# Decoder step on one core: one tick later for the samples' first probability transposes and first value product

## The reference, cut to what matters

```python
def forget_attn_prompt(q, k, v, c):          # 16 heads, 528 rows
    ...
        s = jnp.einsum('nqhd,nkhd->nhqk', qb, kp).astype(jnp.float32) * ATTN_SCALE
        s = s + cb[..., None] - ct[:, :, None, :]
        s = jnp.where(kpos[None, :] <= qpos[:, None], s, NEG_INF)
        p = jax.nn.softmax(s, axis=-1)
        return jnp.einsum('nhqk,nkhd->nqhd', p.astype(vp.dtype), vp)

def forget_attn_sample(q, k_new, v_new, c_new, k_past, v_past, c_past):   # 8 samples
    ...
    p = jax.nn.softmax(jnp.concatenate([s_past, s_new], axis=-1), axis=-1)
    out = jnp.einsum('nhqk,nkhd->nqhd', p[..., :past].astype(v_past.dtype), v_past)
    return out + jnp.einsum('nhqk,nkhd->nqhd', p[..., past:].astype(v_new.dtype), v_new)
```

## Time and profile before

| | |
|---|---|
| time, median of 3 runs | 1491.27 us (1487.19 to 1493.64) |
| the profiled execution's own time | 1491.63 us |
| its span in the trace | 1489.8 us |
| PE busy | 1319.4 us, 89% |
| weight loads busy, beside PE | 1025.3 us, 69% |
| DVE, ACT, POOL busy | 34%, 21%, 12% |
| rounds 4 to 7 in the trace | about 780 to 1036 us |
| mean granted PE clock | 0.931 of full |

### The profile page before, as it was taken

The page is one execution under the profiler, slowest core; times in us unless marked ns, Lnnn a source line. Parts: engine busy times, 40 slices in busy tenths (PEclk is TensorE's granted clock), DMA queues, the critical chain, the costliest instruction groups (busy, mean ns, idle before and its releaser), DMA issues.

```text
span 1489.8 us, 37491 instructions
## 1 busy us (share of the span) xinstructions
PE 1319.4 (89%) x16016; PEld 1025.3 (69%) x16016; DVE 499.4 (34%) x1121; ACT 308.5 (21%) x726; POOL 172.5 (12%) x206
## 2 busy tenths in 40 slices
PE   5989999999667889998989999998995899999990
PEld 5888888888534766766665656555454898888870
DVE  4340000000056445464646766664124100000003
ACT  3121000000133221313133543434110001000010
POOL 1012000000031011101021211210000300000002
PEclk9889999999978999999999988999995899999995
DMA  9259999999988759797978996984363599999965
GB/s 304 100 217 319 384 382 383 384 384 392 358 300 294 244 193 364 263 372 252 376 239 268 308 315 229 334 294 153 118 242 118 149 362 387 388 386 384 385 240 197
DMA packets 148138, 437.93 MB, mean 294 GB/s; under 512 B 21383, under 2 KB 52168, under 8 KB 139055
## 3 DMA queue, kind: packets, MB, share of 16 engines
q1 hardware_dynamic: 99319, 367.64, 67.3%
q10 hardware_dynamic: 37744, 38.88, 7.8%
q0 software_dynamic: 10960, 29.80, 6.7%
HBM read 406.38 MB, written 30.24 MB: 293 GB/s over the span
## 4 chain that ended last, share of the span: by engine, by line
PE 48%; DMA 24%; issue 12%; DVE 6%; ACT 3%; SPq 3%; POOL 2%; ACTq 1%; POOLq 0%; DVEq 0%
DMA W<-in_w_up 17%; PE PS L1217 8%; PE PS L1027 5%; PE PS L1352 5%; PE PS L1023 4%; PE PS L1058 4%; PE PS L1053 4%; DMA out_k_prompt<-W 2%; PE PS L964 2%; PE PS L1296 2%; PE PS L1258 2%; PE PS L1304 2%; PE PS L1316 2%; PE PS L956 1%; DMA W<-in_cache_v 1%
## 5 line engine op out<-in xcount | busy, mean ns | idle before, releaser
L1023 PE MATMUL PS<-W,KV 128*32 128x384 f32 x3072 | 344.2, 489 | 16.4 <-DMA W<-in_w_up 12.0
L1027 PE MATMUL PS<-W,KV 128*32 128x128 f32 x3072 | 347.3, 274 | 0.0
L1027 PEld LDWEIGHTS PS<-W,KV 128*32 128x32 f32 x3072 | 334.9, 110 | 1.6
L1217 PE MATMUL PS<-W 128*128 128x256 f32 x768 | 185.4, 397 | 0.7 <-ACT KV L1611 0.7
L2034 DVE TENSOR_TENSOR KV<-KV,PS 128x384 f32<-128x384 f32 x32 | 17.7, 554 | 495.3 <-PE PS L1039 477.2
L1053 PE MATMUL PS<-W,KV 128*32 128x384 f32 x1536 | 176.0, 495 | 5.9 <-ACT KV L1523 5.9
L1058 PE MATMUL PS<-W,KV 128*32 128x128 f32 (+1 forms) x1024 | 176.0, 331 | 0.0
L1217 PEld LDWEIGHTS PS<-W 128*128 128x128 f32 x768 | 149.4, 200 | 32.2 <-issue 10.1
L1023 PEld LDWEIGHTS PS<-W,KV 128*32 128x32 f32 x3072 | 141.8, 110 | 23.4 <-DMA W<-in_w_up 17.9
L2158 DVE STREAM_TRANSPOSE KV<-KV 128x1024 f32<-128x1024 f32 x128 | 154.8, 1225 | 4.5 <-DMA KV<-in_cache_k 4.5
L1058 PEld LDWEIGHTS PS<-W,KV 128*32 128x32 f32 x1024 | 102.7, 110 | 16.5 <-issue 0.7
(11 more groups left out here) (278 smaller groups left out, 1507.5 us busy)
## 6 DMA issues: line engine op xcount, KB each, us to landing
W<-in_w_gate SPq DMA_DIRECT2D x32, 2048.0 KB, 15.7
W<-in_w_up SPq DMA_DIRECT2D x32, 2048.0 KB, 22.2
W<-in_w_down SPq DMA_DIRECT2D x32, 2048.0 KB, 11.7
KV<-in_cache_k SPq DMA_DIRECT2D x256, 256.0 KB, 5.5
W<-in_cache_v SPq DMA_DIRECT2D x128, 512.0 KB, 7.6
yd<-KV ACTq DMA_DIRECT2D x32, 288.0 KB, 7.1
W<-in_w_kvf SPq DMA_DIRECT2D x4, 2048.0 KB, 16.8
W<-in_w_kvf ACTq DMA_DIRECT2D x8, 1024.0 KB, 8.8
```

The source lines that it names most:

```text
L1023: pe.matmul(PS[32 * q:32 * q + 32, bank, 0:WIDE], x, w[:, k, 0:WIDE], start=(k == 0), stop=(k == KC - 1), tile_position=(0, 32 * q), skip_ ...
L1027: mm = pe.matmul(PS[CAP:P, bank, P * q:P * q + P], x, w[:, k, WIDE:FF], start=(k == 0 and q == 0), stop=(k == KC - 1), tile_position=(0, C ...
L1217: mm = pe.matmul(PS[:, b, 0:GW], XTP[:, k, t * P:t * P + P], WB[j % 2][:, k, :], start=(k == 0), stop=(k == KC - 1))
```

## The change

The transposes of parts 0, 1 and 2 move from ticks 24, 25 and 26 to ticks 25, 26 and 27, and `values(i, 0)` moves from tick 27 to tick 28. Parts 3 and 4 stay. This holds for rounds 4 to 7 alone. No instruction is added, removed or altered. With the steps move their copies on ACT, the take-out of the product on DVE, and one reciprocal on DVE that stands at the tick `PT[0]`. The lists of POOL and SP stay as they are, though SP's load of chunk 2 waits for the product that moved.

```diff
-    PT = (24, 25, 26, 28, 29)
+    PT = (25, 26, 27, 28, 29)
     NEW = 30
-    LO = (27,)
+    LO = (28,)
```

## The result

The changed kernel takes 1499.61 us, the median of 20 runs (1483.61 to 1508.09). The kernel before takes 1491.05 us in 20 runs (1485.37 to 1498.79). The ratio is 1.0049, with an interval of 1.0030 to 1.0069. On the 1491.27 us shown ahead of the prediction that makes 1498.6 us. The forecast was 1492.5 us. So the change costs 7 to 9 us and not 0.9. The range ended at 1498.5 us: the median of 1499.61 us lies 1.1 us above that, and by the ratio it is 0.1 us. The prediction had given 88% to a time within 0.5% of 1491.27 us, and the ratio of 1.0049 lies just inside that. This is luck, since neither the path nor the sum behind the 88% led to it.

A forecast was written before the change was run, and what follows sets the result against it. PE, the busiest engine at 89%, was taken to bound the kernel. A late group (2.4 us), less 0.9 for `new_keys` and 0.6 for cached values, added 0.9 us to 1491.63, giving 1492.5 us; range 1486 to 1498.5 us.

The forecast's parts named there:

- The stop in one piece: PE before the fourth head's first `s_step`: idle about 2.6 us unbroken, with part 0's transposes directly behind.
- The queue late by one group, 0.6 us a round: PE from part 2 on, behind `v_step`: everything one group of four late, 0.6 us a round, 2.4 us in all.
- `new_keys` gives back 0.3 us a round: Wait of `new_keys` for part 4's copy in rounds 4, 5 and 6: 0.39 us falls to 0.1, returning 0.9 us.
- The product does not bound the third `s_step`: DVE's take-out of the later value product ends about 1.3 us before the third `s_step`; cost taken as 0.
- Rival three: DVE's take-out falls behind a key transpose, third `s_step` waits 1.2 us each round: 1497.3 us, 7% chance.
- The wait for cached values gets shorter by 0.6 us: Start of round 7: chunk 2's later load helps chunk 1, cutting PE's 1.48 us stop by 0.6 us, between 0.3 and 1.5.
- From exponent to exponent under 1 us at the same clock: Sign: from `s_step` at one round's start to the next, difference under 1 us where the clock is the same.
- ACT costs nothing: ACT's copies of the moved parts: same-size copies swap places and part 2's goes behind `ot`, at no cost.
- What the clock can add: Low clock after each exponent: 3.4 us in round 4, 17.2 in round 5, the difference costing 6.9 us where PE limits.
- rival two: The unbroken 2.6 us stop keeps the clock down longer in one more round, adding 6.9 us: 1499.4 us, 7% chance.
- What the low level costs: Price of time at 1.2 GHz where PE is the limit: 13.8 us at the low level costs 6.9 us.
- the sum without the gain on cached values: The order's own cost on PE: 2.4 us for the late group less 0.9 us for `new_keys`, 1.5 us.

The follow-up runs named there:

- the kernel with the parts late: The changed kernel with the value product back at tick 27, parts 0, 1 and 2 still one tick later; ratio 1.0042 to the kernel before.
- part 0 back: The changed kernel with part 0's transposes back at tick 24, parts 1 and 2 and the value product still late; ratio 1.0027 to the kernel before.
- the filled pairs: Discarded matmuls in the stops, changed kernel against kernel before: 11 against 5 and 2 (0.9995, 0.9992), 18 against 9 and 4 (0.9990, 0.9987).

## Why the prediction was right and wrong, step by step

**The stop in one piece: right.** It was to be 2.6 us with the transposes behind it. It is 2.60 us in three rounds. In round 5 it is 1.05 us. There PE was at half speed ahead of it and came later.

**The queue late by one group, 0.6 us a round: right.** This can be read cleanly in rounds with the same clock. In round 4 of the kernel before, the third `s_step` came 11.83 us after the first and `new_keys` 13.37 us after it. Round 6 of the changed kernel has the same clock of 0.97 over its whole length:

```profile
961.72 1.09 PE L1296 MATMUL PS<-W 65*128 65x144 f32 x6 [2.60 <-ACT W L1767]
...
974.04 1.15 PE L1296 MATMUL PS<-W 65*128 65x512 f32 x4
...
975.35 0.74 PE L1242 MATMUL PS<-V,W 32*32 32x32 f32 x64 [0.16 <-ACT W L1798]
```

The third `s_step` comes 12.32 us after the first, 0.49 us later than before. The term said 0.6.

**`new_keys` gives back 0.3 us a round: right.** It stops 0.16 us instead of 0.39 and starts 13.63 us after the first `s_step`, 0.26 us later than before. The forecast for this point was 0.6 - 0.3 = 0.3 us.

**The product does not bound the third `s_step`: right.** DVE's take-out, 0.42 us, ends well ahead of the `s_step`: the list of waits has none for it in any round. Rival three was not there.

**The wait for cached values gets shorter by 0.6 us: wrong.** The row of the changed kernel in place of the earlier trace rows:

```profile
982.23 1.93 PE L1258 MATMUL PS<-W 128*32 128x256 f32 x32 [1.82 <-DMA W<-in_cache_v]
```

The stop has grown by 0.34 us, outside the bounds of 0.3 to 1.5 us in the other direction. In the second trace of the changed kernel it is not there at all. So from one execution to the next it moves by more than I wanted to gain, and the term should have been 0 with its range to both sides. The issues of chunk 1 in the changed kernel, for the earlier trace rows:

```profile
L642 SPq DMA_DIRECT2D W<-in_cache_v x4: 333/333/337, 961.5 to 963.5; - x4
...
DMA to landing us min/median/max: 7.8/11.4/18.6
```

The Trainium skill, "DMA: Bandwidth & Descriptors", section "Queues, rings and completion order", spoke for the smaller gain, and these two traces agree: chunk 2 was issued 11.3 us behind chunk 1 instead of 10.6, and chunk 1's slowest page took 18.6 us in both. The prediction held against that section that a later page landed first; the section itself says that a later transfer may finish its write before an earlier one, so that was no objection. With 0 the sum is +1.5 us.

**From exponent to exponent under 1 us at the same clock: right.** It was 63.8 us for round 6 before and is 64.4 us now, both at 0.97.

**ACT costs nothing: right at the slow clock, incomplete at the fast one.** In round 5 of the changed kernel PE is at the full clock behind the exponent's stop, and then it stops for ACT:

```profile
901.84 2.59 PE L1316 MATMUL PS<-W 16*64 16x128 f32 x18 [1.50 <-ACT W L1758]
```

In round 7 of the kernel before, also at the full clock there, that stop was 0.55 us. In round 4 of either kernel, at half speed, there was none. A faster PE only comes earlier to a copy that is not there yet, and that takes back a part of what a better clock gives.

**"What the clock can add": this is the step that failed.** It said "Nothing in the kernel makes round 5 another case than 4 or 6. A stop that moves against the clock may find such a stretch or miss it", and rival two, one more long stretch, got 7%. Which round is hit is indeed not fixed. How much is hit depends on the order. The product's later place adds some: 10.2 +- 3.4 us at the low level between the kernel with the parts late and the changed one, and -9.6 +- 2.9 us the other way, where it stands earlier. With the parts early it was only +3.2 +- 3.8 us, which fits less well. The later parts add some as well, +8.2 +- 2.7 us with the product at its old place. How much of that is the unbroken stop is not shown: with part 0 late alone it was +6.0 +- 3.5 us, and with part 0 back and all else late still +13.9 +- 3.8 us.

The long stretches shown all end at the product. In round 5 of the kernel before:

```profile
899.68 3.45 PE L1258 MATMUL PS<-W 128*32 128x256 f32 x32
903.07 0.94 PE L1296 MATMUL PS<-W 65*128 65x400 f32 x2
```

The `s_step` behind it takes 0.94 us, the full clock's time. It is the same in round 4 of the changed kernel and of the one with part 0 back. A product that comes later then means a longer stretch. The other traces have exceptions, though: with the product late alone the stretch of round 5 ends at 899.3, ahead of the product at 900.19, and with part 0 late alone the clock is full from 844.9 in round 4, ahead of the product at 847.69. So the product is where most long stretches end, not where all do, and why the clock comes back there the runs don't say.

Rival two had the size, 1499.4 us, and a part of the cause: more time at the low level, but not by the stop in one piece alone. Its time lay 0.9 us outside the stated range, which was said to take in most of it. The evidence held against it, the 3.35 us in one piece of the earlier trace rows with only 3.4 us at the low level behind, was from round 1, whose work behind the stop is another. What follows the stop counts as well, and I didn't compare that.

**What the low level costs: the size was off.** The prediction took half a microsecond for each one. Over 249 runs of all these kernels, each against the mean of its own kernel, it is 0.295 +- 0.024 us. For the second measurement of the changed kernel the means differ by 8.0 us. Its 18.4 us at the low level are then 5.4 of them, and 2.6 us are left for the order, where the sum without the gain on cached values has 1.5 us. In the profiled pair the fit is closer with a half: 13.7 us more at the low level are 6.9 of the 9.0 us, and 2.1 are left. The slope of 0.295 tells how the time goes with the low level among runs of one kernel. It isn't shown to be a price, since a run that waits longer for its transfers could lose both time and clock. Taken as a price, it gives the clock 5.4 of 8.0 us, two thirds of the loss, with an error of about 1 us on either number; by the filled pairs the clock has some 6 to 8 us. The exact share stays open. What can bring it below a half is in the rows shown: PE at the full clock waits 1.50 us for ACT and up to 3.3 us for value pages.

## What to carry to other kernels

Before moving work out of a stop, write down what the granted clock does behind that stop in every round, and compare the rounds by what runs between the stop and the clock's return. A reordering that costs PE 0.3 us a round by its own sum cost some 2 us a round here, most of it through the clock. When a trace shows such stretches, filling the stop with a few discarded matmuls is a cheap test of what they cost; the gain is bounded by the engines that PE then waits for, so look for those first.

## What was unexpected of the hardware

- The same two stops, 1.24 and 0.71 us with 0.66 us of work between, were followed by 3.4 us at the low level in round 4 of the kernel before and by 13.5 us in round 4 of the kernel with part 0 back. In the long stretches PE is busy for most of the time: 20.68 of 22 us. The longest had begun before the stop that the change made.
- A few microseconds of discarded matmuls in the stops, 2.6 us a round in the changed kernel, took 33 us off the time at the low level (+18.4 to -14.2 us against the kernel before).
- Filling one stop made the next one as long as 1.50 us, and the clock fell behind that one instead.
- Among runs of one kernel, a microsecond more at half the clock went with 0.3 us more time, though the engine is busy for 89% of it.
